# A gated linear-attention scan: decayed queries and keys built in place from block products instead of exponentials

## The reference, cut to what matters

```
S_t = diag(f_t) S_{t-1} + k_t v_t^T,   o_t = S_t^T q_t
```

```
scores[t, s] = sum_d q[t, d] * k[s, d] * exp(b[t, d] - b[s, d])      for s <= t
o = scores @ v + (q * exp(b)) @ S
S = exp(b_last) * S + (k * exp(b_last - b))^T @ v
```

## Time and profile before

| what | value |
|---|---|
| median of 2 runs | 1418.55 us (1417.76 to 1419.33) |
| the profiled execution | 1420.56 us |
| its span, first to last instruction | 1418.8 us |
| busy PE / DVE / ACT / POOL | 1401.1 / 1031.2 / 704.5 / 226.1 us |
| share of the ending chain on PE | 93% |
| scan, first score to the tail's first matmul | 418.23 to 558.71 us |

### The profile page before, as it was taken

How to read it: one execution, slowest core, us unless ns; L and a number is a source line. 1 busy time by engine, 2 the same in 40 slices (tenths; PEclk the granted TensorE clock), 3 DMA queues, 4 the chain that set the end, 5 groups by cost and what they waited for, 6 DMA issues and landing times.

```text
span 1418.8 us, 20665 instructions
## 1 busy us (share of the span) xinstructions
PE 1401.1 (99%) x7683; PEld 1171.1 (83%) x7683; DVE 1031.2 (73%) x1522; ACT 704.5 (50%) x1309; POOL 226.1 (16%) x239
## 2 busy tenths in 40 slices
PE   9999999999999999999999999999999999999998
PEld 8877888888878998888888888888888888888886
DVE  7594545562148997368988999999999686577567
ACT  6343456422258896258653344343435444454455
POOL 4000001101038885010000000000000254400000
PEclk9999999999999999999999999999999999999999
DMA  7431323544623332645342344334327765424223
GB/s 241 105 74 30 45 80 116 154 112 108 166 72 108 121 120 83 216 149 184 105 126 82 119 136 139 111 104 160 108 89 259 240 195 196 135 82 134 90 61 148
DMA packets 153251, 181.06 MB, mean 128 GB/s; under 512 B 21241, under 2 KB 92095, under 8 KB 153152
## 3 DMA queue, kind: packets, MB, share of 16 engines
q1 hardware_dynamic: 153152, 179.74, 40.8%
HBM read 130.43 MB, written 49.28 MB: 127 GB/s over the span
## 4 chain that ended last, share of the span: by engine, by line
PE 93%; DVE 3%; ACT 1%; issue 1%; DMA 1%; POOL 0%; SPq 0%; DVEq 0%; ACTq 0%; POOLq 0%
PE psum L2468 9%; PE psum L2470 9%; PE psum L2469 9%; PE psum L2407 5%; PE psum L2408 5%; PE psum L2409 5%; PE psum L674 4%; PE psum L676 4%; PE psum L675 4%; PE psum L2380 4%; PE psum L2381 4%; PE psum L2382 4%; PE psum L1373 3%; PE psum L734 3%; PE psum L732 3%; PE psum L733 3%
## 5 line engine op out<-in xcount | busy, mean ns | idle before, releaser
L166 DVE TENSOR_TENSOR w_wlo<-w_raw,w_whi 128x1024 fp32r<-128x1024 f32 x66 | 86.8, 1317 | 228.1 <-ACT w_whi L151 228.0
L151 ACT ACTIVATE w_whi<-w_raw 128x1024 fp32r<-128x1024 f32 x66 | 69.7, 1058 | 175.4 <-PE psum L2382 79.0
L3201 DVE TENSOR_TENSOR g_slot<-w_raw,g_slot 128x512 fp32r<-128x512 f32 x77 | 69.5, 902 | 51.6 <-ACT g_slot L2775 51.5
L2775 ACT ACTIVATE g_slot<-w_raw 128x512 fp32r<-128x512 f32 x77 | 48.7, 632 | 104.8 <-PE psum L2409 99.6
L674 PE MATMUL psum<-h_hi,w_whi 128*128 128x512 f32 x256 | 100.6, 393 | 0.0
L676 PE MATMUL psum<-h_hi,w_wlo 128*128 128x512 f32 x256 | 99.7, 390 | 0.0
L675 PE MATMUL psum<-h_lo,w_whi 128*128 128x512 f32 x256 | 99.7, 389 | 0.0
L3459 POOL TENSOR_TENSOR mixed_home<-mixed_home 128x512 f32<-128x512 f32 x11 | 16.0, 1455 | 507.0 <-DMA mixed_home<-in_w_down 505.0
L2380 PE MATMUL psum<-w_whi,m_hi 128*128 128x512 f32 x224 | 87.8, 392 | 0.0
L2382 PE MATMUL psum<-w_whi,m_lo 128*128 128x512 f32 x224 | 87.2, 389 | 0.0
L2381 PE MATMUL psum<-w_wlo,m_hi 128*128 128x512 f32 x224 | 87.2, 389 | 0.0
(11 more groups left out here) (446 smaller groups left out, 3967.0 us busy)
## 6 DMA issues: line engine op xcount, KB each, us to landing
w_raw<-in_w_up SPq DMA_DIRECT2D x39, 512.0 KB, 4.0
w_raw<-in_w_in SPq DMA_DIRECT2D x36, 512.0 KB, 6.2
s_rows<-pair_work SPq DMA_DIRECT2D x11, 1024.0 KB, 4.1
w_raw<-s_rows SPq DMA_DIRECT2D x44, 256.0 KB, 2.7
g_rows<-pair_work SPq DMA_DIRECT2D x18, 512.0 KB, 2.6
w_raw<-g_rows SPq DMA_DIRECT2D x33, 256.0 KB, 4.2
w_raw<-in_w_out SPq DMA_DIRECT2D x16, 512.0 KB, 4.1
mixed_home<-in_w_down SPq DMA_DIRECT2D x32, 256.0 KB, 4.4
```

## The change

The factors are no longer exponentials. Queries and keys are multiplied in place, level by level. `Front.pool_spans` makes, once and on POOL, products of f over blocks of 2, 4, ..., 128 positions (`spans`, 4064 floats on each partition), in place of ACT's Ln and DVE's running sum. In the scan q is first multiplied by f (`pool_begin`). After the score of level n is read, the queries in the upper half of each block of 2m are multiplied by the product over the lower half (`dve_grow`), and the keys in the lower half by the product over the upper half (`pool_grow`); the next level multiplies these same tiles. After the last level q and k are already q exp(b) and k exp(b_last - b), so that the separate tiles go.

With it: scores of level 0 to 5 are done in blocks of 32 positions (four matmuls for each head), 6 in blocks of 64, 7 in one. `y32`, `dt32` and `dx` are cut to the 64 x 64 blocks that matter. ACT takes over the copies after `dt32`/`dt64`, the placing of score levels 6 and 7, the query step of the last level and the scaling of outputs by the norm (`act_scale`); the gate is a multiplication of its own, on DVE for the HGRN2 heads and on POOL for the others (`gate_outputs`). The states' decays move to POOL (`pool_keep`, `pool_hkeep`), and DVE only adds. Query tiles are all put through Silu as they come; the split of the last one (`act_last`, `act_late_silu`) goes. The scores have two score tiles in turn, and the PSUM banks are dealt anew.

The new lists run from c = 0 to 8 and handle two chunks at a time. For a middle c (sN is the score of level N of chunk c, sN' of chunk c+1):

- PE: s4, oh(c-1), dt64, s0', turn(c-1), s5, solve, s1', hd(c-1), s6, y32', gd, og, s2', dt32', dx', s7, mix_h(c-1), y64', s3', mix_g(c-1), ks'.
- DVE: rhs, grow 3, place 4, place 0', grow 4, place 5, grow 0', place 1', inverse(c-1), grow 5, hstate(c-1), grow 1', place 2', state, gate_h(c-1), dx', mix_h(c-1), grow 2', place 3', mix_g(c-1).
- POOL: grow 3, begin', grow 4, grow 0', grow 5, grow 1', gate_g(c-1), grow 6, grow 2', keep, hkeep(c-1).
- ACT: y64 copy, dt64 copy, squares_h(c-1), keys(c-1), root(c-1), vn, scale_h(c-1), scale_g(c-1), place 6, y32' copy, squares_g, dt32' copy, place 7, grow 6, mix_h(c-1), mix_g(c-1).
- Before the loop PE does, for chunk 0: s0, solve, s1, gd, s2, og, y32 of chunk 1, s3, dt32, dx and y64 of chunk 1.

A score of level n waits for both grow steps of level n-2, that is, for DVE and POOL after the score before it. The diff, cut to its core:

```diff
+    def pool_spans(self, pool):
+        pool.wait_ge(self.s["bounded"], 2 * NH)
+        self.multiplied.wait(pool, ("slab", Slabs.QUADS - 1))
+        for n in range(1, LEVELS + 1):
+            if n > 1:
+                pool.wait_ge(self.s["spanned"], n - 1)
+            lower, upper = (self.spans(n - 1, slice(0, SEQ >> (n - 1)), side) for side in range(2))
+            pool.tensor_tensor(self.k.spans[n][:], lower, upper, ALU.mult).then_inc(self.s["spanned"], 1)
...
-        for lv in range(3):
-            self.scan.act_exp(act, 0, lv)
-        act.wait_ge(s["summed"], NH)
-        self.act_last(act, 0, ACT.Silu)
-        for lv in range(3, 6):
-            self.scan.act_exp(act, 0, lv)
-        self.act_last(act, 1, ACT.Copy)
...
+    def spans(self, c, lv, side):
+        width, m = P >> lv, 1 << lv
+        return self.front.spans(lv, slice(c * width, (c + 1) * width), side).unsqueeze(3).broadcast_to([P, NH, width // 2, m])
...
+        for c in range(NT + 1):
+            if c < NT - 2:
+                self.sp_xt(sp, c + 2)
+            if c < NT:
+                self.sp_gate(sp, c, 0)
+                self.sp_gate(sp, c, 1)
+            if 0 < c < NT:
+                self.sp_v(sp, c)
+            if c < NT - 1:
+                self.sp_kd(sp, c + 1)
+                self.sp_at(sp, c + 1)
+            if c < NT - 2:
                 self.sp_lt_x(sp, c + 2)
+    def sp_gate(self, sp, c, g):
+        if c:
+            sp.wait_ge(self.s[("h_gated", "g_gated")[g]], c)
+        self.load_rows(sp, ("h_gate", "g_gate")[g], c, g * DG, self.gate[g])
...
+    def pe_halves(self, pe, key, bank, left, right, side):
+        out = self.banks.open(pe, key, bank)
+        for h in range(NH):
+            for half in range(2):
+                rows = slice(half * 2 * SB, (half + 1) * 2 * SB)
+                cols = slice(rows.start + side * SB, rows.start + (side + 1) * SB)
+                ins = pe.matmul(self.hs(out, h)[rows, cols], left(h)[rows, rows], right(h)[rows, cols], start=True, stop=True)
...
-        return max(64, 1 << n) if n < LEVELS else P
+        return max(SB, 1 << n)
...
+            self.grown(pe, self.q_grown, c, n - 1)
+            self.grown(pe, self.k_grown, c, n - 1)
+        m = 1 << (n - 1)
+        out = self.banks.open(pe, ("score", c, n), self.SCORE_BANK[n])
+        for h in range(NH):
+            for b in range(P // size):
+                keys = slice(b * size, (b + 1) * size - m)
+                queries = slice(b * size // 2, (b + 1) * size // 2)
+                ins = pe.matmul(self.packed(out)[keys, h, queries].rearrange("p (n m) -> p n m", m=m), kk[:, h, keys],
+                                self.half(q[:, h, b * size:(b + 1) * size], m, 1), start=True, stop=True)
...
+    def act_grow(self, act, c):
+        lv = LEVELS - 1
+        self.done(act, ("score", c, lv + 1))
+        for h in range(NH):
+            here = self.front.q[:, h, c * P + (1 << lv):(c + 1) * P]
+            ins = act.activation(here, here, ACT.Copy, scale=self.k.spans[lv][:, h, 2 * c:2 * c + 1])
...
+    def dve_grow(self, dve, c, lv):
+        self.done(dve, ("score", c, lv + 1))
+        here = self.level(self.front.q, c, lv, 1)
+        dve.tensor_tensor(here, here, self.spans(c, lv, 0), ALU.mult).then_inc(self.q_grown[c % 2], 1)
...
+    def gate_outputs(self, eng, c, g):
+        self.banks.released(eng, (("oh", "og")[g], c))
+        eng.wait_ge(self.s[("h_gate_in", "g_gate_in")[g]], (c + 1) * 16)
+        here = self.on[:, g * DG:(g + 1) * DG]
+        eng.tensor_tensor(here, here, self.gate[g][:], ALU.mult).then_inc(self.s[("h_gated", "g_gated")[g]], 1)
...
+        self.done(pool, ("score", c, 0))
+        here = self.part(self.front.q, c)
+        pool.tensor_tensor(here, here, self.part(self.front.f, c), ALU.mult).then_inc(self.s["q_begun"], 1)
...
+        self.done(pool, ("score", c, lv + 1))
+        here = self.level(self.front.kk, c, lv, 0)
+        pool.tensor_tensor(here, here, self.spans(c, lv, 1), ALU.mult).then_inc(self.k_grown[c % 2], 1)
...
```

More of the change, by code:

```diff
@@ L1252 @@
 class Scan:
[L1254 to L1257, removed]
+    SCORE_BANK = (2, 0, 7, 6, 0, 6, 2, 5)
+    BANK_OF = {"oh": 5, "dt64": 1, "turn": 3, "solve": 7, "hd": 1, "y32": 3, "gd": 6, "og": 4, "dt32": 0, "dx": 3, "mix_h": 1, "y64": 2, "mix_g": 7, "ks": 3}
+    DT_ROWS, Y64_FROM, Y64_ROWS = (slice(0, P - SB), slice(0, 2 * SB)), slice(0, 2 * SB), slice(2 * SB, P)
     FIRST_BANK_OF = {"solve": 5, "y32": 4, "dx": 5, "dt32": 6, "y64": 4, "dt64": 6}
@@ L1372, in pe_products @@
         for h in range(NH):
-            ins = pe.matmul(columns(self.hs(out, h)), left(h)[:, rows], columns(right(h)), start=True, stop=True)
+            ins = pe.matmul(columns(self.hs(out, h)), left(h)[inner, rows], columns(right(h)[inner]), start=True, stop=True)
         self.multiplied.mark(ins, key)
@@ L1425, in pe_score @@
         kk, q = self.part(self.front.kk, c), self.part(self.front.q, c)
[L1426 to L1438, removed]
+        size = self.block_of(n)
+        if n == 0:
             if c == NT // 2:
                 self.front.queries(pe, 1)
-            out, size = self.banks.open(pe, ("score", c, n), self.SCORE_BANK[n]), self.block_of(n)
+            out = self.banks.open(pe, ("score", c, n), self.SCORE_BANK[n])
             for h in range(NH):
@@ L1642, in act @@
         self.front.finished(act)
[L1643 removed]
         self.act_vn(act, 0)
[L1645 to L1648 removed]
+        self.act_inverse(act, 1, 0)
+        self.act_squares(act, 0, 1)
+        self.act_dt(act, 1, 0)
+        self.act_inverse(act, 1, 1)
+        for c in range(NT + 1):
+            if 2 <= c < NT:
+                self.act_inverse(act, c, 1)
+            if 0 < c < NT:
+                self.act_dt(act, c, 1)
@@ new lines, in pool @@
+    def pool(self, pool):
+        self.front.finished(pool)
+        self.pool_begin(pool, 0)
+        self.pool_grow(pool, 0, 0)
+        self.pool_grow(pool, 0, 1)
+        self.pool_grow(pool, 0, 2)
+        for c in range(NT + 1):
+            if c < NT:
+                self.pool_grow(pool, c, 3)
+            if c < NT - 1:
+                self.pool_begin(pool, c + 1)
+            if c < NT:
+                self.pool_grow(pool, c, 4)
+            if c < NT - 1:
+                self.pool_grow(pool, c + 1, 0)
+            if c < NT:
+                self.pool_grow(pool, c, 5)
+            if c < NT - 1:
+                self.pool_grow(pool, c + 1, 1)
+            if c:
+                self.gate_outputs(pool, c - 1, 1)
+            if c < NT:
+                self.pool_grow(pool, c, 6)
+            if c < NT - 1:
+                self.pool_grow(pool, c + 1, 2)
+            if c < NT - 2:
+                self.pool_keep(pool, c)
+            if 0 < c < NT - 1:
+                self.pool_hkeep(pool, c - 1)
```

523 lines of the change are left out of this document (239 added, 284 removed).

## The result

The changed kernel takes 1445.11 us (median of 2 runs, 1443.22 and 1447.00) against 1418.55: a ratio of 1.0188, interval 1.0170 to 1.0206. The forecast was 1422, 1407 to 1436, with 0.93 for "within 2%". The sign of the forecast 3.9 us was right; the amount was 26.6. The profiled execution took 1443.22 us, its span 1441.5.

What follows compares the result with a forecast made beforehand. PE's list was taken as the bound, DVE just behind. Start 441.8, six periods of 17.3 and end 16.0 gave +2.9 us; 1.0 for the clock made +3.9: 1422.5 at the median, range 1407 to 1436.

Steps and rivals of the forecast that it cites:

- the charge for the clock: Start and end: fewer matmuls at half clock, but an end wait of about 2 us; 1.0 us more, between 0 and 6.
- rival 3: Scan: gaps on PE in every period keep the clock at half; +50 us, 1470; chance 0.05.
- The wait at mix_h: Each scan period: PE waits 1.1 us for DVE's gate_h, queued behind grow 1', place 2' and state.
- v: Scan: v's load, queued behind the gates on SP, reaches oh late; 0.3 us a period charged, ends 0 and 1.0.
- PE's own work: Scan period after the change: PE's matmuls and tile changes take 15.9 us, ends 15.4 and 17.8.
- Rival 2: Scores s0 to s5: only two narrow tiles run at a time; +1.4 us a period, 1432 to 1437; chance 0.2.
- The changes between kinds of narrow tile: PE's list, 5 in a period: 0.1 us each, 0.5 in all, taken between nothing and 0.2.
- Rival 4: In-place steps with a repeated operand cost as much as 512 elements on DVE and POOL; +10 us, 1432; chance 0.07.
- The bound of the old period: Scan before the change, about 17.5 us a period: PE's list taken as the bound, with DVE just behind.
- rival 1: Scan: DVE was the bound, so PE then runs at its own 15.4 us without wait; -12 us, 1407; chance 0.2.
- The start: Before the loop: y32 of chunk 1 waits for x until 427.50, bringing s4 of chunk 1 to 441.8.
- The end: Last chunk: a chain through og, squares_g, place 7 and grow 6 to oh(7); 16.0 us with v late, 13.57 before.

Runs made afterwards that it cites:

- gate early: Changed kernel with DVE's gate_h(c-1) moved right behind hstate(c-1), ahead of grow 1', place 2' and state: 1426.1 us, ratio 1.0060.
- both moves: Changed kernel with gate_h moved earlier on DVE and the load of v issued ahead of the two gates on SP: 1419.33 us, ratio 1.0016.
- PE relieved of 0.7 us a period: Kernel before with only scores of level 0 to 4 (and 5) in four blocks of 32 positions instead of two of 64: 1420.66 us, ratio 1.0014.
- a better order: Changed kernel with gate_h and v early, plus four more reorderings on DVE, at the start and in the last chunk: 1412.38 us, ratio 0.9962.
- the kernel before with its wait: Kernel before with DVE's norm and gate of outputs moved behind place 4 and the next chunk's level 0 difference: 1432.35 us, ratio 1.0094.
- v early: Changed kernel with the load of v(c) issued ahead of the two gates on SP: 1436.22 us, ratio 1.0145.

## Why the prediction was wrong, step by step

- **The step that failed** is the charge for the clock: "I charge 1.0 more for the clock, between 0 and 6", and behind it rival 3's point of decision, "from the point at which waits in a period reach the 2.4 us". The kernel before had a fall behind 2.4 us of waiting, and I took that length as the point. Waits of 1.29, 1.38 and 1.27 us were enough, though not each time. The kernel before had shown it: the 0.87 in the last row is a second fall, 3.4 us at half behind waits of 1.38 and 1.02, the very "1.4 and 1.0 us" of the sum:

```profile
548.49 1.13 PE L1373 MATMUL psum<-s_g_rn,s_xt 128*128 128x128 f32 x8 [1.38 <-DVE s_xt L1691]
551.13 1.09 PE L1455 MATMUL psum<-ident,s_normed 128*128 128x128 f32 x4 [1.02 <-DVE s_normed L1784]
```

  The mechanism was rival 3's, with 0.05; its size (all of a period at half, 1470) was as wrong as the charge, since the clock came back after 6.9 us. A fall costs 3.4: about 17 us in the six periods, and about 2 more in the end, where 1.0 had been charged for all. Without it the six periods would be 104, against 103.8 forecast; part of that match is luck, since at half clock the wait for v was mostly hidden. The Trainium skill describes such a pattern in "TensorE: Matmul & The Clock Gate", A second HAM failure mode: in another kernel, short pauses of PE between groups of matmuls that make the clock swing. The trace agrees, at 1.00 and 0.51 in turn.
- **The wait at mix_h was right**: 1.29 us in every period, 1.1 forecast, for the gate behind grow 1', place 2' and state. The difference: gate_h takes 1.30 us where POOL's gate_g runs beside it, and 0.68 with the gate early, where it doesn't; I had 0.75. The Trainium skill's "GPSIMD Engine Reference", Key points, says that POOL and DVE contend when DVE has two inputs in SBUF, which this is. The trace agrees, 1.30 against 0.68.
- **v was mis-sized**: 0.3, ends 0 and 1.0; at full clock it is 1.3 to 1.5 in the periods shown (19.1 against 17.7), more in others (2.08), and 3.88 at the end. Seven loads now leave together, and v lands 4.4 us after its issue, not in the 2.6 to 3.6 of the earlier trace rows:

```profile
s_h_gate<-gate_rows SPq DMA_DIRECT2D x5, 256.0 KB, 2.6
s_g_gate<-gate_rows SPq DMA_DIRECT2D x5, 256.0 KB, 3.0
s_h_v<-gate_rows SPq DMA_DIRECT2D x5, 256.0 KB, 4.4
```

- **PE's own work was right**: 15.9 forecast, 15.96 busy in a period with both moves. Rival 2 falls: 31 further loads of a score take 0.34 - 0.11 us, 7.4 ns each, half of the 14.5 of the earlier trace rows. The changes between kinds of narrow tile are not free: eight loads of dt64 at 0.058 end at 481.71, s0' starts at 481.86, 0.15 us, where 0.1 had been taken; the same reckoning gives 0.12 to 0.15 from s6 to y32', s2' to dt32' and dx' to s7. The trace agrees there with the rule of the Trainium skill on which the prediction draws ("TensorEngine Tiling (Array Packing)", Tiling Modes).

```profile
481.25 0.54 PEld L1379 LDWEIGHTS psum<-s_xt,inverse_y 64*64 64x64 f32 x8
481.86 0.35 PEld L1452 LDWEIGHTS psum<-hgrn_q,hgrn_k 128*32 128x32 f32 x32
...
484.24 0.34 PEld L1466 LDWEIGHTS psum<-hgrn_q,hgrn_k 128*31 128x31 f32 x32
```

- **Rival 4 falls**: steps in place on 256 elements cost 0.58 us on DVE and 0.85 on POOL, with the operand repeated; 0.45 and 0.85 had been taken.

```profile
L1917 POOL TENSOR_TENSOR hgrn_k<-hgrn_k,h_span 128x256 f32<-128x256 f32 x36 | 30.7, 853 | 39.4 <-PE psum L1466 39.2
L1766 DVE TENSOR_TENSOR hgrn_q<-hgrn_q,h_span 128x256 f32<-128x256 f32 x30 | 17.4, 579 | 20.6 <-PE psum L1466 20.0
```

- **The bound of the old period** was not PE alone. PE relieved of 0.7 us a period (busy 16.62) gained nothing (1420.66), so the other engines held the 17.4 beside it. (In its profiled execution the clock fell once, behind a wait of 1.46 us and in none of the periods compared.) With them relieved too, and in a better order, the period is 15.7. That is the size of rival 1's term, 17.5 - 15.4 a period; the new waits and the clock lay over it.
- **The start** was better than forecast, s4 of chunk 1 at 439.63 and not 441.8: x landed by 426.19 and y32 didn't wait, though PE lost 2.38 us to DVE's memsets, which I had overlooked. **The end** was 19.7 us, not 16.0: the wait for v of 3.88 us, and half clock for 3.4 us behind it.

Start -2.2, periods 121.1 - 103.8 = +17.3, end +3.7: that is the 18.8 between +21.7 and +2.9.

What stays open: why the half clock lasts 6.9 us here and 3.4 on the kernel before with its wait, and why at equal waits some periods escape (one of six after, three of six in v early, two of seven on the kernel before). No run gives a length from which a wait costs the clock.

## What to carry to other kernels

Where an engine list is dense, ask of each wait that a change adds to PE whether its clock survives it, look for falls in the trace of before and the waits ahead of each of them, and charge the work behind as well; the row to look for is PEclk by windows of a period. Relieved engines show nothing in the time until the lists are put in order again: here the same instructions took 1445 us and, in another order, 1412. And test two overlapping causes in all four combinations: each removed alone gave 5 and 9 us, both together 20.

## What the runs showed of the hardware beyond that

Matmuls without use held the clock: 11.0 us off the new kernel with v early, 8.8 off the old one with the late norm. A DVE product of two SBUF tiles took 0.68 us alone and 1.30 beside a POOL product. Waits of 0.41 and 0.67 us in one period left the clock at 1.00; of those from 1.2 to 2.1 us some did and some didn't, those of 1.29 in one and the same execution.
